# GpSimd normalizes, VectorE copies: one change in two softmax attentions

## What is computed

```python
# first block: chunk of 64 queries, own chunk and up to 8 before it
scores = jnp.where(valid, q @ k + bias, -jnp.inf)
probs = jax.nn.softmax(scores, axis=-1)
out = probs @ v
# second block: windows of 128 keys to both sides, one sink logit for each head
m = jnp.maximum(logits.max(-1), sink_f)
p = jnp.exp(logits - m[..., None])
denom = p.sum(-1) + jnp.exp(sink_f - m)
o = (p @ vs) / denom
```

## Time and profile before

| | us |
|---|---|
| median of 3 runs | 2365.34 |
| lowest, highest | 2362.56, 2367.77 |
| the profiled execution | 2365.04 |
| its span | 2363.2 |
| TensorE busy in the span | 2309.6 (98%) |
| VectorE busy | 1715.6 (73%) |
| ScalarE busy | 872.1 (37%) |
| GpSimd busy | 1019.4 (43%) |

### The profile page before, as it was taken

The page is one execution under the profiler, slowest core; times in us unless marked ns, Lnnn a source line. Parts: engine busy times, 40 slices in busy tenths (PEclk is TensorE's granted clock), DMA queues, the critical chain, the costliest instruction groups (busy, mean ns, idle before and its releaser), DMA issues.

```text
span 2363.2 us, 34880 instructions
## 1 busy us (share of the span) xinstructions
PE 2309.6 (98%) x12272; PEld 1980.0 (84%) x12272; DVE 1715.6 (73%) x3188; ACT 872.1 (37%) x1386; POOL 1019.4 (43%) x1080
## 2 busy tenths in 40 slices
PE   7999999999999999999998899999999999999998
PEld 5885788888888887678898898888899999999998
DVE  5467743332389986867999898588787778888886
ACT  3137222222232243832434455444433333333333
POOL 4530555656655556155541001344455433444440
PEclk9999999999999999999999999999999999999999
DMA  5320223333323323122232467999999989999993
GB/s 170 97 64 28 72 89 98 98 98 105 102 96 98 98 89 112 42 72 84 90 100 88 172 256 265 297 370 320 323 336 333 326 298 315 327 346 332 329 350 126
DMA packets 213107, 437.69 MB, mean 185 GB/s; under 512 B 111760, under 2 KB 116368, under 8 KB 209936
## 3 DMA queue, kind: packets, MB, share of 16 engines
q1 hardware_dynamic: 65376, 235.44, 29.8%
q0 software_dynamic: 39440, 142.10, 16.7%
q10 hardware_dynamic: 108192, 58.92, 8.6%
HBM read 401.81 MB, written 30.41 MB: 183 GB/s over the span
## 4 chain that ended last, share of the span: by engine, by line
PE 75%; DVE 15%; issue 4%; POOL 4%; ACT 1%; DMA 1%; DVEq 0%; POOLq 0%; ACTq 0%; SPq 0%
PE bank L2370 21%; PE bank L1831 16%; PE bank L1833 16%; PE bank L1832 16%; POOL lo L656 3%; DVE ohg L1731 2%; PE bank L1989 1%; DVE lo L1670 1%; PE bank L2000 1%; PE bank L1976 1%; DVE oh L1727 1%; DVE oh L1728 1%; PE bank L2311 1%; DVE idx L1629 1%; DVE scb L1622 1%
## 5 line engine op out<-in xcount | busy, mean ns | idle before, releaser
L656 POOL TENSOR_TENSOR lo<-raw,hi 128x256 fp32r<-128x256 f32 (+1 forms) x740 | 631.4, 885 | 772.2 <-ACT hi L775 553.8
L1831 PE MATMUL bank<-inH,hi 128*128 128x512 f32 (+1 forms) x2112 | 778.1, 368 | 30.0 <-DVE inL L1198 14.7
L1833 PE MATMUL bank<-inH,lo 128*128 128x512 f32 (+1 forms) x2112 | 769.5, 364 | 0.0
L1832 PE MATMUL bank<-inL,hi 128*128 128x512 f32 (+1 forms) x2112 | 769.1, 364 | 0.0
L1831 PEld LDWEIGHTS bank<-inH,hi 128*128 128x128 f32 x2112 | 398.5, 189 | 82.0 <-issue 16.8
L1832 PEld LDWEIGHTS bank<-inL,hi 128*128 128x128 f32 x2112 | 398.9, 189 | 45.0 <-issue 0.2
L1833 PEld LDWEIGHTS bank<-inH,lo 128*128 128x128 f32 x2112 | 398.4, 189 | 42.7
L775 ACT ACTIVATE hi<-raw 128x1024 fp32r<-128x1024 f32 x236 | 248.0, 1056 | 403.9 <-PE bank L1833 389.7
L1146 ACT ACTIVATE hi<-raw 128x1024 fp32r<-128x1024 f32 x204 | 215.6, 1057 | 197.9 <-PE bank L2370 197.8
L711 POOL DMA_INDIRECT rows<-rows_u,expert x128 | 188.9, 1476 | 188.1 <-DVE dots L1773 167.1
L1764 DVE TENSOR_TENSOR lo<-raw,hi 128x1024 fp32r<-128x1024 f32 x208 | 253.3, 1219 | 19.8 <-ACT hi L1146 18.6
(11 more groups left out here) (331 smaller groups left out, 2759.7 us busy)
## 6 DMA issues: line engine op xcount, KB each, us to landing
raw<-stream SPq DMA_DIRECT2D x440, 512.0 KB
Gd<-gates ACTq DMA_DIRECT2D x32, 768.0 KB
gates<-stage_a ACTq DMA_DIRECT2D x12, 1024.0 KB, 4.5
gates<-stage_b ACTq DMA_DIRECT2D x12, 1024.0 KB, 4.3
tbl<-gqa ACTq DMA_DIRECT2D x8, 384.0 KB, 3.3
A<-spilled POOLq DMA_DIRECT2D x8, 384.0 KB
xT<-x SPq DMA_DIRECT2D x4, 512.0 KB, 9.0
h_rep<-h_tok POOLq DMA_DIRECT2D x16, 128.0 KB
```

What stands on the lines that cost most here:

```text
L656: ins = pool.tensor_tensor(lo[:, r, part], raw[:, r, part], hi[:, r, part].bitcast(F32), ALU.subtract)
L1831: pe.matmul(bank, wh, xh, start=start, stop=False)
L1832: pe.matmul(bank, wh, xl, start=False, stop=False)
L1833: return pe.matmul(bank, wl, xh, start=False, stop=stop_)
```

## The change

In both attentions GpSimd normalizes both halves of each pair, after VectorE's reciprocal. VectorE, in its place, copies the second half's transposed block out of PSUM for pair p-2, at the end of iteration p, and runs one iteration more. ScalarE copies the first half only. The semaphore of the copies is split in two, `turned_sb` for the first half and `turned_sb_odd` for the second, and `inverse` is added from VectorE to GpSimd. GpSimd's first loop over slots is cut in two so that the first attention's normalizations stand behind slot S_OUT + 2. In the second attention each sink is written in front of the normalization of the pair before it.

```diff
--- before.py
+++ after.py
@@ -466,7 +466,7 @@
         sb_out = sem("sb_out")
 
         att = [{n: sem(f"{n}{a}") for n in ("score", "logit", "probs", "normed", "turned",
-                                           "turned_sb", "mixed", "head_out", "sunk")} for a in (1, 2)]
+                                           "turned_sb", "turned_sb_odd", "inverse", "mixed", "head_out", "sunk")} for a in (1, 2)]
         tbl_in = [[sem(f"tbl_in{a}{b}") for b in (0, 1)] for a in (1, 2)]
         y_sb = sem("y_sb")
         y_sq_act = sem("y_sq_act")
@@ -656,22 +656,37 @@
                     ins = pool.tensor_tensor(lo[:, r, part], raw[:, r, part], hi[:, r, part].bitcast(F32), ALU.subtract)
                 ins.then_inc(lo_done, 1)
 
-            def sinks():
+            def normalize(st, v):
+
+                s, w = st["s"], st["pairs"][v]
+                pool.wait_ge(s["inverse"], v + 1)
+                for half in (0, 1):
+                    pr = st["pr"][:, v % PAIRS_PR, half, :w["n"]]
+                    pool.tensor_scalar(pr, pr, st["sm"][:, v % 2, 4, half:half + 1], None, ALU.mult).then_inc(s["normed"], 1)
+
+            def sink(p, w):
 
                 s = att[1]
-                for p, w in enumerate(pairs2):
-                    if p >= PAIRS_PR:
-
-                        pool.wait_ge(s["turned"], 2 * (p - PAIRS_PR + 1))
-                    else:
-                        pool.wait_ge(s["score"], 1)
-                    less = gn[:, w["sink"]].unsqueeze(2)
-                    pool.tensor_copy(pr2[:, p % PAIRS_PR, :, w["n"]:w["n"] + 1], less).then_inc(s["sunk"], 1)
+                if p >= PAIRS_PR:
+
+                    pool.wait_ge(s["turned"], 2 * (p - PAIRS_PR + 1))
+                else:
+                    pool.wait_ge(s["score"], 1)
+                less = gn[:, w["sink"]].unsqueeze(2)
+                pool.tensor_copy(pr2[:, p % PAIRS_PR, :, w["n"]:w["n"] + 1], less).then_inc(s["sunk"], 1)
 
             for r in range(RING):
                 low(r, r, D)
             first = S_IN2 // RING + ADD_LAG + 1
-            with pool.Fori(1, first) as i:
+            with pool.Fori(1, S_OUT // RING) as i:
+                for r in range(RING):
+                    low(i * RING + r, r, PIECE)
+            for r in range(AHEAD):
+                low(S_OUT + r, r, PIECE)
+            for v in range(len(pairs1)):
+                normalize(stage1, v)
+            low(S_OUT + AHEAD, AHEAD, PIECE)
+            with pool.Fori(S_OUT // RING + 1, first) as i:
                 for r in range(RING):
                     low(i * RING + r, r, PIECE)
             for r in range(RING):
@@ -689,7 +704,11 @@
                     low(i * RING + r, r, PIECE)
             for r in range(AHEAD):
                 low(S_WO + r, r, PIECE)
-            sinks()
+            for p, w in enumerate(pairs2):
+                sink(p, w)
+                if p:
+                    normalize(stage2, p - 1)
+            normalize(stage2, len(pairs2) - 1)
             low(S_WO + AHEAD, AHEAD, PIECE)
             with pool.Fori(S_WO // RING + 1, S_PEER // RING) as i:
                 for r in range(RING):
@@ -829,9 +848,8 @@
                         if v >= 2:
 
                             act.wait_ge(s["mixed"], v - 1)
-                        for half in (0, 1):
-                            act.wait_ge(s["turned"], 2 * v + half + 1)
-                            act.activation(st["pT"][:, v % 2, half, :w["n"]], B[6 + half][:, :w["n"]], ACT.Copy).then_inc(s["turned_sb"], 1)
+                        act.wait_ge(s["turned"], 2 * v + 1)
+                        act.activation(st["pT"][:, v % 2, 0, :w["n"]], B[6][:, :w["n"]], ACT.Copy).then_inc(s["turned_sb"], 1)
                     v = p - 4
                     if v >= 0 and v % TT == TT - 1:
                         w = pairs[v]
@@ -1256,7 +1274,7 @@
             def attention(st, amid=None):
                 s, pairs, sm = st["s"], st["pairs"], st["sm"]
                 n = len(pairs)
-                for p in range(n + 1):
+                for p in range(n + 2):
                     if amid:
                         amid(p)
                     if p < n:
@@ -1281,15 +1299,18 @@
                     k = (p - OUT_LAG) // TT
                     if st is stage2 and p % TT == OUT_LAG % TT and 0 <= k < OUT_SPLITS:
                         split_out(k)
-                    if p >= 1:
+                    if 1 <= p <= n:
                         v = p - 1
                         w, b = pairs[v], v % 2
                         dve.wait_ge(s["probs"], v + 1)
-                        chain(dve.reciprocal(sm[:, b, 4, :], sm[:, b, 2, :]))
-                        for half in (0, 1):
-                            pr = st["pr"][:, v % PAIRS_PR, half, :w["n"]]
-                            ins = dve.tensor_scalar(pr, pr, sm[:, b, 4, half:half + 1], None, ALU.mult)
-                            ins.then_inc(s["normed"], 1)
+                        dve.reciprocal(sm[:, b, 4, :], sm[:, b, 2, :]).then_inc(s["inverse"], 1)
+                    if p >= 2:
+                        v = p - 2
+                        w = pairs[v]
+                        if v >= 2:
+                            dve.wait_ge(s["mixed"], v - 1)
+                        dve.wait_ge(s["turned"], 2 * v + 2)
+                        dve.tensor_copy(st["pT"][:, v % 2, 1, :w["n"]], B[7][:, :w["n"]]).then_inc(s["turned_sb_odd"], 1)
 
 
             x_of = lambda k: xT[:, k, :]
@@ -1983,7 +2004,7 @@
                         w = pairs[v]
                         for half in (0, 1):
                             if v >= 1:
-                                pe.wait_ge(s["turned_sb"], 2 * v + half - 1)
+                                pe.wait_ge(s[("turned_sb", "turned_sb_odd")[half]], v)
                             pe.wait_ge(s["normed"], 2 * v + half + 1)
                             for c in range(0, w["n"], P):
                                 m = pe.transpose(B[6 + half][:, c:c + P], st["pr"][:, v % PAIRS_PR, half, c:c + P], ident)
@@ -1991,7 +2012,8 @@
                     v = p - 3
                     if v >= 0:
                         w = pairs[v]
-                        pe.wait_ge(s["turned_sb"], 2 * v + 2)
+                        pe.wait_ge(s["turned_sb"], v + 1)
+                        pe.wait_ge(s["turned_sb_odd"], v + 1)
                         if w["group"] >= 2 and v % TT == 0:
                             pe.wait_ge(s["head_out"], w["group"] - 1)
                         nb = w["n"] // P
```

## The result

| | before | after |
|---|---|---|
| median, same chip | 2363.95 | 2402.06 |
| lowest, highest (4 runs each) | 2362.27, 2367.77 | 2396.16, 2407.18 |
| the profiled execution | 2365.04 | 2396.16 |
| its span | 2363.2 | 2394.4 |

The account below looks back on a forecast made before the run. TensorE was taken to bound the first attention and unsplit groups, a chain of waits the six split groups of the second. 6 x (0.42 + 0.69) = 6.7, + 0.2 + 1.2 + 0.7 - 0.5 = +8.3 us: 2373, range 2366 to 2380.

Parts of the forecast that it names:

- (1): Price n of one GpSimd normalization: 0.55, 0.73, 0.92 us at 256, 384, 512 columns; at 384 between 0.39 and 1.01.
- 2n + 0.5: GpSimd's way from reciprocal to exponentials: two scalings of n each, sink copy and hand-overs, 1.96 us at 384 columns.
- (4): Second attention, reciprocal to pair 3's exponentials: the sink queued behind pair 1's normalization holds them, +0.69 us a split group.
- (7): First attention: copy before the logits lengthens a nearly full circle; sum 1.2 us, none if cheap, 3 to 4 if dear.
- (2): VectorE gives two normalizations for one copy, 0.2 us a pair; ScalarE gives 0.438; counts only by place in the circle.
- (3): VectorE's copy of the fourth pair stands before pair 2's logits, uncovered: +0.42 us in the second attention's circle.
- (5): TensorE cannot get back the 0.31 us a group lost to waits; the two groups without a split cost +0.1 each.
- (6): TensorE's added wait before the values: priced at nothing, hidden in the queue; at worst 48 x 0.05 = 2.4 us.
- (9): GpSimd's other work, its subtractions before and behind the attentions, stays as now: nothing.
- (8): Ends of the second attention: opening +0.7 us, as sinks come behind first normalizations; end -0.5 from moving the second copy.
- The ports: Shared SBUF port lock: scalings could block the split, 6 x 1.5 = 9 us more; no meeting expected, none added.
- dear scaling: Rival: GpSimd scaling costs the subtraction's rate, 1.01 us at 384 columns; +13.5 us, 2379; chance 0.11.

Follow-up runs that it names:

- tt_scale: Changed kernel with GpSimd's scaling as a product of two tensors, the reciprocal repeated along the columns; 2375.76 us, ratio 1.0043.
- copy_only: Against the changed kernel, VectorE normalizes again and still copies the second half, GpSimd only writes sinks; 2378.96 us, ratio 1.0056.
- half-and-half kernel: Kernel before, with GpSimd normalizing only the second half as a two-tensor product, and the sink written before the previous pairs' normalization; 2370.44 us, ratio 1.002.

## Why the prediction was wrong, step by step

- **(1) Prices: the step that failed, and with it the main term, 2n + 0.5 of step (4).** "By values moved" gave 0.73 at 384 and "the upper end is the subtraction" gave 1.01; measured are 1.26. I took it that an instruction with fewer operands can't cost more than one with more. tt_scale shows the reasoning itself was not far off for an instruction of the same kind: the two-tensor product with a repeated operand costs 1.67 ns a column, below the subtraction's 2.15. The scaling is another kind, at 2.50. No row of the trace had that kind on this engine, so the subtraction was a neighbour and not a bound. Of the 31 us about 20 (ratios 1.0128 and 1.0043) go with the difference between the two forms, 0.42 at 384 columns and 0.20 to 0.52 at the others. With 1.26 put into the prediction's own sum, (4) would be +1.74, the six split groups 6 x (0.42 + 1.74) = 13.0, the two others about 2.8 and the ends 1.2: an estimate of 17 for the second attention, where 19.0 were measured. For the first the prediction had 3 to 4 at its high price, and 10.8 were measured. By the numbers the price thus explains nearly all that was missing in the second attention; the rest is a missing circle in the first (7).
- The Trainium skill, "GPSIMD Engine Reference", section "Engine selection", holds one-input elementwise work to be roughly at line rate, by which I had an estimate of 0.51. The runs contradict it: 1.26 for the scaling at 384 columns. The measurement decides.
- **(2) Load.** In the second attention VectorE got 8.2 us emptier over 32 pairs (63.50 busy before, 55.27 after), 0.26 a pair where 0.2 was told. That it counts only in the circle holds too, and copy_only shows the other side: without the saving the engine is full.
- **(3) The copy in front of the logits.** Right in place, 0.28 to 0.29 instead of 0.42, because records of VectorE overlap by 0.08 and a hand-over became shorter.
- **(4) From the reciprocal to the exponentials.** The wait came as told, 28 times and 30.4 us, and decided nothing but once, at the start of the attention. What came last for TensorE was GpSimd's own queue: normalization of pair 1, sink, normalization of pair 2. That way stands in the prediction only in the dear rival, as a load that "would fill GpSimd". As a worked circle: 4 scalings and the sink (0.13), and 5.74 of the rest of the chain after (10.77 - 5.03). The other circle, of tt_scale, has 2 scalings and 7.82 (9.44 - 1.62). At my 0.73 the second one leads with 9.28, near what I forecast; from about 1.0 on the first leads, and each further tenth costs 0.4 a group instead of 0.2.
- **(5), (6), (9).** TensorE gave nothing back. Its added wait does not appear in the chain as a term. Outside the attentions nothing became longer but the 2 us at the lower clock behind the first, a term that the sum did not have.
- **(7) First attention: 11 us instead of 1.2, and of 3 to 4 at most.** From its first to its last transpose it is 9.7 longer (40.6 against 30.9). Six scalings in a row, of 256, 384 and 512 columns, take 7.35, and 3.28 stand between. At my price they would be 4.4 (2 x (0.55 + 0.73 + 0.92)), the circle 7.7 and TensorE's 8.53 longer. So it is the price again, with a circle that the prediction had not drawn: it looked at pair 3's second half and not at the row of them. The copy adds about 2 by itself (copy_only, 33.0 against 30.9), which was also above the 1.2.
- **(8) Ends.** They were not measured by themselves and stay open. From the first split to the sixth, five periods, the second attention takes 12.8 us more than before (starts of the split's second instruction: 981.75 to 1036.63 against 966.03 to 1008.13), 1.0 of it in the group at the lower clock. The other 6.2 of its 19.0 lie before the first split and behind the last.
- **The ports.** I expected no meeting of the split with GpSimd's scalings, and there is none: after, the split's second instruction takes 0.70 (1003.29), as before (999.71). That a scaling can be held was seen in the half-and-half kernel: VectorE 1.03 instead of 0.43 beside GpSimd's 0.83. The Trainium skill, "SBUF — State Buffer", section "Who interferes with whom", calls this an exclusive lock, and the trace agrees.

Of the rivals, dear scaling was the right one (chance 0.11), and its 1.01 and +13.5 were still too low, because its end was set by the same neighbour. It also set GpSimd's 8 us of load against a group of 9.5, where its own sum gives 8.42 + 1.67 = 10.1.

## What to carry to other kernels

A price for an instruction that no row shows is not bounded by a different instruction with more operands; if the step rests on it, leave the upper end open and work out from which price another circle takes over. When work moves to an idle engine, add up what stands in a row in that engine's queue within one period, with everything that must happen before its next order comes, and not only what each single result is needed for. An engine that is waited for 30 us can still be off the circle: look whether what it delays is done before the circle needs it. A run that takes the wait away shows this only if it puts no other wait in. And compare the groups of one execution with each other: one that is longer than its like can be at another clock.

## What the runs showed of the hardware

On GpSimd a scaling by one factor a row (f32, in SBUF) took 0.60, 0.92, 1.26 and 1.56 us at 128, 256, 384 and 512 columns, and 1.18 at 384 with a constant. The same result as a product of two tensors, the second one repeated, took 0.40, 0.61, 0.83 and 1.04. VectorE takes 0.42 for it at 384, and 1.03 when it starts just behind GpSimd's product. TensorE's lower level (1.2 GHz) cost 1.0 to 1.1 us in a group where it was granted (11.8 against 10.77), although the group was full of waits. A mean clock of 0.87 instead of 0.96 over the whole attention moved the median by less than the runs can tell (2396.81 and 2396.22).
